# A diffusion backbone kernel on one core: row products dealt differently, context keys normed by head pairs, a tile closed in halves, buffers in another order

## What is computed

```python
for l in range(DEPTH):                       # l = 0: conv and spatial gating; l = 1: conformer and attention
    ada_x = (silu(c) @ w_ada[l] + b_ada[l])  # six vectors of 1024: shift, scale, gate, twice
    hx = modulate(rms_norm(x, norm1_g[l]), ada_x[0], ada_x[1])
    yx = mixer(hx, hc, w_in[l], w_out[l], ...)
    x = x + ada_x[2] * yx
    h2 = modulate(rms_norm(x, norm2_g[l]), ada_x[3], ada_x[4])
    x = x + ada_x[5] * peer(h2, wq[l], subkeys[l], u_tab[l], v_tab[l])
    # layer 0 does the same for the context stream

def diff_attend(q, k, v, lam):               # 4 heads of 2 x 64 keys, 128 values each
    s = einsum('bqhmd,bkhmd->bhmqk', q, k) * 64 ** -0.5
    p = softmax(s)
    return einsum('bhqk,bkhe->bqhe', p[:, :, 0] - lam * p[:, :, 1], v)

def peer(h, wq, subkeys, u_tab, v_tab):      # per token: 8 heads x 16 of 16384 experts
    idx, g = top16_of_products(h @ wq, subkeys)
    act = gelu(einsum('td,thkd->thk', h, u_tab[idx]))
    return einsum('thk,thkd->td', g * act, v_tab[idx])
```

## Time and profile before

| | before |
|---|---|
| time, median of 3 runs (lowest, highest) | 2312.71 us (2308.45, 2313.47) |
| the profiled execution's own time | 2306.4 us |
| its span | 2304.6 us |
| busy: PE, DVE, POOL, ACT | 2060.9, 1597.9, 997.0, 953.3 us |
| moved by DMA | 943.22 MB, mean 409 GB/s |
| of it by gathers (queue q0) | 805.36 MB |

### The profile page before, as it was taken

How to read it: one execution, slowest core, us unless ns; L and a number is a source line. 1 busy time by engine, 2 the same in 40 slices (tenths; PEclk the granted TensorE clock), 3 DMA queues, 4 the chain that set the end, 5 groups by cost and what they waited for, 6 DMA issues and landing times.

```text
span 2304.6 us, 23920 instructions
## 1 busy us (share of the span) xinstructions
PE 2060.9 (89%) x6960; PEld 1126.1 (49%) x6960; DVE 1597.9 (69%) x3904; ACT 953.3 (41%) x2795; POOL 997.0 (43%) x868
## 2 busy tenths in 40 slices
PE   8998998999998888988999998798799978888887
PEld 7785554555564444444554554346546423333222
DVE  3865778967766668888866667855686885666654
ACT  2024444543334444444454334533554443444433
POOL 0003444344444544444445445420344545455663
PEclk9999999999999999999999999999899999999999
DMA  9979999999999999999999999986799999999997
GB/s 405 426 296 388 426 420 427 427 426 427 426 427 426 427 426 426 427 426 427 419 426 427 427 427 427 426 314 284 306 425 426 426 427 426 428 426 427 427 427 319
DMA packets 133618, 943.22 MB, mean 409 GB/s; under 512 B 14832, under 2 KB 18544, under 8 KB 19568
## 3 DMA queue, kind: packets, MB, share of 16 engines
q0 software_dynamic: 110592, 805.36, 83.2%
q1 hardware_dynamic: 22896, 136.35, 14.2%
HBM read 940.60 MB, written 1.05 MB: 409 GB/s over the span
## 4 chain that ended last, share of the span: by engine, by line
PE 38%; DMA 34%; DVE 13%; issue 6%; POOL 5%; ACT 3%; SPq 0%; POOLq 0%; DVEq 0%; ACTq 0%
DMA uv<-uv_dram,stage_idx 32%; PE psum L1016 21%; PE psum L819 9%; DVE uv L1619 5%; POOL uv L1090 5%; PE psum L801 4%; PE psum L959 1%; DVE h L1321 1%; DMA uv<-in_dram 1%; DMA uv<-ada_dram 1%; ACT diag L1264 1%; PE psum L991 1%; PE psum L734 1%; ACT small L1260 1%; DVE work L1427 1%
## 5 line engine op out<-in xcount | busy, mean ns | idle before, releaser
L1016 PE MATMUL psum<-uv,diag 128*128 128x512 f32 x3072 | 1438.7, 611 | 185.1 <-ACT diag L1264 176.7
L1090 POOL DMA_INDIRECT uv<-uv_dram,stage_idx x768 | 965.2, 1257 | 1013.3 <-PE psum L1016 773.1
L1619 DVE CUSTOM_DVE_ANT_0 uv<-uv,h 128x1024 f32<-128x1024 f32 x768 | 932.8, 1225 | 521.6 <-DMA uv<-uv_dram,stage_idx 512.2
L1016 PEld LDWEIGHTS psum<-uv,diag 128*128 128x128 f32 x3072 | 567.1, 193 | 943.8 <-issue 522.8
L1258 ACT ACTIVATE small<-small 128x1 f32<-128x1 f32 x768 | 155.1, 202 | 1016.9 <-DVE small L1619 1015.8
L1264 ACT ACTIVATE diag<-const,small 128x128 f32<-128x128 f32 x768 | 308.4, 402 | 25.1
L819 PE MATMUL psum<-hT,wring 128*128 128x256 f32 (+1 forms) x1344 | 270.9, 355 | 0.0
L819 PEld LDWEIGHTS psum<-hT,wring 128*128 128x128 f32 x1344 | 233.5, 191 | 60.8 <-issue 36.4
L1260 ACT ACTIVATE small<-small,gw 128x1 f32<-128x1 f32 x768 | 226.2, 295 | 24.9
L1076 POOL COPY stage_idx<-idx 128x8 uint32<-128x8 uint32 x96 | 31.6, 329 | 264.2 <-DVE idx L1590 263.6
L1110 ACT ACTIVATE work<-psum 128x256 f32<-128x256 f32 (+2 forms) x127 | 48.3, 383 | 130.1 <-PE psum L819 100.6
(11 more groups left out here) (220 smaller groups left out, 1276.9 us busy)
## 6 DMA issues: line engine op xcount, KB each, us to landing
uv<-ada_dram SPq DMA_DIRECT2D x27, 1024.0 KB, 19.3
wring<-wq_dram SPq DMA_DIRECT2D x26, 1024.0 KB, 11.3
wring<-in_dram SPq DMA_DIRECT2D x23, 1024.0 KB, 9.1
uv<-uv_dram,stage_idx POOLq DMA_INDIRECT x768, 21.2
uv<-in_dram SPq DMA_DIRECT2D x11, 1024.0 KB, 23.2
uv<-ada_t_dram SPq DMA_DIRECT2D x10, 1024.0 KB, 25.8
wring<-ada_dram SPq DMA_DIRECT2D x9, 1024.0 KB, 23.0
uv<-out_w_dram SPq DMA_DIRECT2D x4, 1024.0 KB, 21.0
```

The source lines that it names most:

```text
L1016: last = mm(acc[:, b, :], diag[:, s % DIAGS, :], uv[:, s % RING, D + 512 * b:D + 512 * (b + 1)], start=(c == 0), stop=(c == NSEL - 1))
L1090: nc.gpsimd.indirect_dma_start(out=uv[:, r, :], out_offset=None, in_=tables[stage // 2], in_offset=bass.IndirectOffsetOnAxis(ap=places[:, ...
L1619: v.tensor_tensor_reduce(out=uv[:, r, 0:D], in0=uv[:, r, 0:D], in1=h2[:, row_of[stage], t, :], scale=1.0, scalar=0.0, op0=ALU.mult, op1=AL ...
```

## The change

It has five parts.

1. The buffers are allocated in another order, `uv`, `wring`, `x`, `h2`, `hT`, `work`, `vx` and so on by size, `const` and the small ones last. The built program places 2,048 bytes of DMA scratch and four constants of 32 bytes each ahead of the first buffer, in both kernels. So in each partition `uv` stands at byte 93,440 before (a multiple of 256) and at 2,176 after (128 beyond a multiple of 1,024, and of 256); `wring` at 41,664 before (192 beyond a multiple of 256) and at 92,288 after (128 beyond).
2. In the opening the row products are dealt in three parts: 10 among the first 18 steps of the mixer, 10 among the rest with the gates, and 4 among the four steps `out_rows`.
3. In the gap the keys of tile 1 are normed and turned by pairs of heads, each as soon as its block is there; the scores of heads 0 and 1 wait for the first pair alone; `vc1` block 0 stands behind these scores, block 1 behind `value` of head 1, `ada_turn` of pair 8 behind that; `ada` pair 8 stands behind the norm of the context tile; `lam` moves to the end of stage 1.
4. A tile is closed in halves: a new semaphore `half_summed` tells that bank 0 is summed while PE works on bank 1, and `acc_free` counts halves.
5. The result leaves in four stores of 128 x 512 instead of two of 128 x 1024.

```diff
+    rows = [step for layer, first, last in ADA_ROWS for step in ada_rows_of(layer, first, last)]
...
-        + deal(deal(mixing[:-4] + [mixing[-4], gates[0], mixing[-3], gates[1]] + mixing[-2:],
-                    [step for layer, first, last in ADA_ROWS for step in ada_rows_of(layer, first, last)]),
-               ada(0, 10, 12) + ada(1, 0, 3))
-        + deal(out_rows(0, 0), ada(1, 3, 4)) + [("mods", 0, 1)] + rms(0, one) + ada(1, 4, 6)[:2] + norm(0, 1)[:1] + ada(1, 4, 6)[2:]
+        + deal(deal(mixing[:-12], rows[:10]) + deal(mixing[-12:-4] + [mixing[-4], gates[0], mixing[-3], gates[1]] + mixing[-2:],
+                                                    rows[10:-4]), ada(0, 10, 12) + ada(1, 0, 3))
+        + deal(out_rows(0, 0), rows[-4:] + ada(1, 3, 4)) + [("mods", 0, 1)] + rms(0, one) + ada(1, 4, 6)[:2] + norm(0, 1)[:1] + ada(1, 4, 6)[2:]
...
-        2: [root] + rms(1, (1,)) + [("idle", 10), ("ada", 1, 8), ("kc_turn", 2, 0), ("norm_ctx", 2, 1)]
-        + [("kc1", 2, b, 0) for b in range(2)] + [("kc_norm", 2, 1), exp, ("vc1", 2, 0, 0), ("ada_turn", 1, 8), ("kc_turn", 2, 1), ("lam", 2)]
-        + [scores[0], scores[1], smax[0], smax[1], soft[0], soft[1], ("vc1", 2, 1, 0), mix[0]]
-        + [p_turn[0], scores[2], mix[1], value[0], smax[2], soft[2], p_turn[1], scores[3], mix[2], value[1], smax[3], soft[3]]
+        2: [root] + rms(1, (1,)) + [("idle", 10), ("kc_turn", 2, 0), ("norm_ctx", 2, 1), ("ada", 1, 8)]
+        + [("kc1", 2, 0, 0), ("kc_norm", 2, 1, 0), ("kc1", 2, 1, 0), ("kc_turn", 2, 1, 0), ("kc_norm", 2, 1, 1), exp]
+        + [scores[0], scores[1], ("kc_turn", 2, 1, 1), ("vc1", 2, 0, 0), smax[0], smax[1], soft[0], soft[1], mix[0]]
+        + [p_turn[0], scores[2], mix[1], value[0], smax[2], soft[2], p_turn[1], scores[3], mix[2], value[1], ("vc1", 2, 1, 0),
+           ("ada_turn", 1, 8), smax[3], soft[3]]
...
+    placed += spread([("lam", 2)], at + 248, at + 250)
...
-                if c == 0 and T:
-                    pe.wait_ge(acc_free, T)
                 pe.wait_ge(diag_ready, s + 1)
                 for b in range(2):
+                    if c == 0 and T:
+                        pe.wait_ge(acc_free, 2 * T - 1 + b)
                     last = mm(acc[:, b, :], diag[:, s % DIAGS, :], uv[:, s % RING, D + 512 * b:D + 512 * (b + 1)],
                               start=(c == 0), stop=(c == NSEL - 1))
+                    if c == NSEL - 1 and b == 0:
+                        last.then_inc(half_summed, 1)
...
-                sp.wait_ge(x_rows_ready, t + 1)
-                sp.dma_start(A["result"][t], x[:, TT + t, :]).then_inc(out_stored, 16)
+                for b in range(2):
+                    sp.wait_ge(x_rows_ready, 2 * t + b + 1)
+                    sp.dma_start(A["result"][t][:, b * 512:(b + 1) * 512], x[:, TT + t, b * 512:(b + 1) * 512]).then_inc(out_stored, 16)
...
-            def kc_norm(stage, t):
-                dve.wait_ge(*taken[("kc0", "kc1")[t]])
-                heads_sum(kc_rows[t], sq[:, 0, :])
-                heads_scale(kc_rows[t], 1).then_inc(kc_normed, 1)
+            def kc_norm(stage, t, pair=None):
+                dve.wait_ge(*taken[("kc0", "kc1")[t], 1 if pair is None else pair])
+                heads = heads_of(pair)
+                cols = slice(heads[0] * P, (heads[-1] + 1) * P)
+                heads_sum(kc_rows[t][:, cols], sq[:, 0, cols])
+                heads_scale(kc_rows[t][:, cols], 1).then_inc(kc_normed, 1)
...
-                v.tensor_tensor(tmp, acc.rearrange("p a b -> p (a b)"), gate_peer[:, :], ALU.mult).then_inc(acc_free, 1)
-                dve.wait_ge(acc_free, T + 1)
...
+                for b, half in enumerate(halves):
+                    if b == 0:
+                        dve.wait_ge(half_summed, T + 1)
+                    else:
+                        dve.wait_ge(uv_used, RING + (T + 1) * NSEL)
+                    v.tensor_tensor(tmp[:, half], acc[:, b, :], gate_peer[:, half], ALU.mult).then_inc(acc_free, 1)
+                    if stage == 2:
+                        dve.wait_ge(acc_free, 2 * T + b + 1)
+                        v.tensor_tensor(row[:, half], row[:, half], tmp[:, half], ALU.add).then_inc(x_rows_ready, 1)
+                if stage < 2:
+                    dve.wait_ge(acc_free, 2 * T + 2)
+                    link(v.tensor_tensor(row, row, tmp, ALU.add))
```

More of the change, by code:

```diff
@@ L404, in sem @@
             return ctx.enter_context(nc.semaphore(name))
+        uv = sb("uv", [P, RING, 2 * D])
+        wring = sb("wring", [P, WRING, BLK_W])
+        x = sb("x", [P, 2 * TT, D])
+        h2 = sb("h2", [P, 2, TT, D])
+        hT = sb("hT", [P, KC, TOK])
+        work = sb("work", [P, 8704])
+        vx = sb("vx", [P, TT, MIX])
+        wst = sb("wst", [P, 8 * P])
+        gate_mix = sb("gate_mix", [P, D])
+        gate_peer = sb("gate_peer", [P, D])
+        keys = sb("keys", [P, 2, SUB_W])
+        diag = sb("diag", [P, DIAGS, P])
         const = sb("const", [P, W_CONST])
-        wst = sb("wst", [P, 8 * P])
         ones = sb("ones", [P, P])
-        x = sb("x", [P, 2 * TT, D])
         silu_c = sb("silu_c", [P, KC, QW])
@@ L661, in last_in, with heads_of @@
             return end - 1 - (end - 1 - place) % RING
+        def heads_of(pair):
+            return tuple(range(HEADS)) if pair is None else (2 * pair, 2 * pair + 1)
         def tile_of(stage, t):
@@ L859, in step, with turn_heads, kc_turn @@
                     token_major(to_act, hcT[t], like or name, like is None, like is None)
-                    taken[name] = (act_took, to_act.n)
+                    taken[name] = taken[name, b] = (act_took, to_act.n)
                 return step
-            def turn_heads(tile):
+            def turn_heads(tile, heads=tuple(range(HEADS))):
                 bank = to_act.open(pe)
-                for h in range(HEADS):
-                    last = turn(bank[:, h * P:(h + 1) * P], tile[:, h * P:(h + 1) * P], ident)
+                for i, h in enumerate(heads):
+                    last = turn(bank[:, i * P:(i + 1) * P], tile[:, h * P:(h + 1) * P], ident)
                 to_act.fill(last)
-            def kc_turn(stage, t):
-                pe.wait_ge(kc_normed, t + 1)
-                turn_heads(kc_rows[t])
-                n["kT"] = to_act.n
+            def kc_turn(stage, t, pair=None):
+                pe.wait_ge(kc_normed, n.up("kc_normed"))
+                turn_heads(kc_rows[t], heads_of(pair))
+                n["kT", pair] = to_act.n
             def qk_turn(stage, i, t):
@@ L1146, in heads_root, with ctx_root, kc_turn @@
                 root(root_heads[:, :], ms_heads[:, :])
-            def ctx_root(*_):
-                root(root_heads[:, 0:8], ms_heads[:, 0:8])
+            def ctx_root(stage, t, pair=None):
+                g = 2 * len(heads_of(pair))
+                root(root_heads[:, 0:g], ms_heads[:, 0:g])
             def ctx_rows(dst):
                 return lambda stage, b, *_: empty(dst[:, b * BLK:(b + 1) * BLK], BLK)
-            def kc_turn(stage, t):
-                empty(kcT[:, :, t * P:(t + 1) * P], 4 * P, a=HEADS)
+            def kc_turn(stage, t, pair=None):
+                heads = heads_of(pair)
+                empty(kcT[:, heads[0]:heads[-1] + 1, t * P:(t + 1) * P], len(heads) * P, a=len(heads))
             def qk_turn(stage, i, t):
@@ L1624, in close @@
                 stage, t = T // TT, T % TT
-                dve.wait_ge(uv_used, RING + (T + 1) * NSEL)
                 dve.wait_ge(*taken["gate", stage, 1])
-                tmp = h2[:, row_of[stage], t, :]
-                v.tensor_tensor(tmp, acc.rearrange("p a b -> p (a b)"), gate_peer[:, :], ALU.mult).then_inc(acc_free, 1)
-                dve.wait_ge(acc_free, T + 1)
-                row = x[:, tile_of(stage, t), :]
-                done = v.tensor_tensor(row, row, tmp, ALU.add)
-                if stage == 2:
-                    done.then_inc(x_rows_ready, 1)
-                else:
-                    link(done)
+                tmp, row = h2[:, row_of[stage], t, :], x[:, tile_of(stage, t), :]
+                halves = [slice(b * 512, (b + 1) * 512) for b in range(2)]
+                for b, half in enumerate(halves):
[10 more added lines that the diff above has]
+                    link(v.tensor_tensor(row, row, tmp, ALU.add))
             v.memset(ones[:, :], 1.0)
```

23 lines of the change are left out of this document (8 added, 15 removed).

## The result

| | before | changed |
|---|---|---|
| median | 2310.58 us (2307.8 to 2313.47, 4 runs) | 2336.84 us (2335.1 to 2338.68, 4 runs) |
| profiled execution: own time, span | 2306.4, 2304.6 | 2335.98, 2334.2 |
| rate of the full stretches | 424 and 426 GB/s | 418 and 421 GB/s |

The ratio is 1.0114 (95% interval 1.0096 to 1.0131): 26 us slower, where I forecast no change and a range up to 2319. Of the times that I had named, that of the rival with 0.04 (2342) lies nearest.

What follows compares the result with a forecast made beforehand. DMA was taken to bound the kernel, so only time where DMA stands could change. Terms -1.5 + 2.3 - 0.9 = -0.1 gave 2306.3 us profiled, 2312.6 against the runs' median of 2312.7; range 2305 to 2319.

Steps and rivals of the forecast that it cites:

- the rival with 0.04: Gathers into uv: unaligned rows of 8192 bytes each cost 128 bytes more, +29 us, 2342; chance 0.04.
- Buffers: 0 us: New buffer places: loads into wring (428 GB/s) and gathers into uv (427) equally fast, so the new offset costs 0.
- the rule: DMA rule of the Trainium skill: a descriptor not starting at a multiple of 256 B fetches from the multiple below.
- Opening: -1.5 us: Opening: first gather 4.0 us sooner, at 162.5, but five gathers instead of six ahead of the wait, +2.5; net -1.5.
- The first rival's other gain: Opening: last out_rows block spared the 0.50 clock, gathers' wait ends 2.0 us sooner, opening wins 3.5; rival's chance 0.25.
- Gap: +2.3 us: Gap: first exponentials 1.3 us sooner, but copies hold those of head 3, losing that and 2.3 us more.
- The rival of the falling clock: Gap: PE stands 3.3 us and its clock falls; gap costs +7.3, whole +4.9, 2317.6; chance 0.18.
- its own condition: Gap: the clock rival decides when PE runs at 0.50 from p_turn of head 0 through vc1 block 1.
- The reason given that waits of 2.5 us do not bring 0.50: Gap: argument against the falling clock; the trace before showed waits of 2.5 us at clock 1.00.
- Tail: -0.9 us: Tail: closing in halves saves 0.6 us, a last store half as large 0.3 us; bounds -0.4 and -1.3.
- 5.0 us after PE's last slot: Tail: sign to look for, the last store in two halves and the end 5.0 us after PE's last slot.
- the sum -0.1: Whole kernel: opening -1.5, gap +2.3 and tail -0.9, with buffers 0, add to -0.1 us.

Runs made afterwards that it cites:

- e1: The kernel before with only the change's order of buffers (uv at byte 2176, 128 beyond a multiple of 256): 2339.35 us, ratio to before 1.0126.
- e4: The kernel before with a 128-byte buffer (ci) placed just ahead of uv, so uv starts 128 beyond a multiple of 256: 2339.98 us, ratio to before 1.0122.
- e7: The kernel before with the 64-byte prec moved behind uv, so uv starts 192 beyond a multiple of 256: 2338.65 us, 1.0134.
- e8: The kernel before with the 96-byte stage_idx placed ahead of uv, so uv starts 96 beyond a multiple of 256: 2339.22 us, 1.0137.
- e3: The changed kernel with a 128-byte buffer (ci) ahead of uv, so uv and wring start at multiples of 256: 2307.55 us, ratio to before 0.9984.
- e5: e3 with the steps of the gap as in the kernel before (one key norm of four heads): 2306.37 us, 0.9988.
- e6: e3 with vc1 block 1 back ahead of the turning of head 0, under the first exponentials; keys still normed by pairs: 2304.17 us, 0.9984.
- e12: e6 with ci and ada_c (896 bytes) ahead of uv, so uv, wring, x, h2, hT, work start at multiples of 1024: 2304.89 us, 0.9979.
- e9: The kernel before with the 64-byte prec ahead of wring, moving wring to a multiple of 256 while uv stays: 2307.46 us, 0.9993.

## Why the prediction was wrong

**Buffers: 0 us. This step failed**, and it alone put the time out of the range. The words were: "at both places the rate is the same, so it should be at 128 beyond too". The rates were read from windows of 7 us and 80 us, and the first can't carry the comparison. The landings in the same trace, 2.481 us apart for 2.447, would have spoken for the rule, as the earlier trace rows seemed to speak against it. The term is +28 us (e1 and e4: +29). The rival had the place, the sign and nearly the size (+29), and I gave it 0.04 on the strength of the faulty reading. That its size fits is in part luck: it took the cost of a row from the 128 bytes of this offset, and e7 and e8 show the same cost at 192 and at 96. A cost that falls on 768 transfers needs evidence at 1% before it is put aside.

**Opening: -1.5 us. Right, within the scatter.** `out_rows` at 123.83 (123.3 forecast), last addition to the end at 141.06 (140.4), the turning at 144.84 (144.3), the first gather at 163.02 (162.5), five gathers ahead. DMA stands some 4 us before 150 (share 0.97), as foreseen. The 21st gather lands 1.7 us earlier in the changed kernel; in the kernels with `uv` at a multiple of 256 and the changed opening (e2, e3, e5, e6, e12) it lands at 227.6 to 230.1, with the old one at 230.5 and 232.3 (before, e9). That is -2 us, with a scatter as large. With `uv` off and the old opening (e1, e4, e7, e8) it lands at 231.2 to 233.3, 2.4 to 4.5 us behind the changed kernel. The first rival's other gain here did not come: the last block behind the wait again ran partly at 0.50 (5.22 us).

**Gap: +2.3 us. Right in mechanism, too small.** The first exponentials came 1.5 us sooner (1.3 forecast), those of head 3 were held by the two copies, and block 1 was the step that did it (e6). But head 3 came 15.7 us behind head 0, not 13.7, and the gap cost +4.0. The rival of the falling clock named what was missing: PE stood 3.11 us (3.3 forecast) and ran at 0.50 behind it, from `p_turn` of head 0 on. By its own condition it did not fully decide: `vc1` block 1 ran at full clock (3.62 us), so it cost some 2 us (15.7 for 13.7) and not 5. The reason given that waits of 2.5 us do not bring 0.50 held in that one trace: behind the same 2.52 us, PE's clock fell in e4, e5, e8 and e9. Against before as a group of traces rather than one, the changed gap is 2 to 6 us dearer.

**Tail: -0.9 us. Right:** -1.0 from the last landing, -1.1 from PE's last slot. The end "5.0 us after PE's last slot" that I gave as a sign does not follow from this sum: it was 5.6 before (2304.6 less 2299.0), so 4.7 was due, and it came at 4.4.

**Pieces that add up.** Without the buffers, the sum -0.1 would have stood: e2, the changed kernel on the old buffers, is at 0.9995 (0.9986 to 1.0005). That is no proof of each piece: the gap was 1.7 us off in the changed kernel and 2.6 in e2, and the time does not resolve that.

## What to carry to other kernels

When a kernel is bound by DMA, the start of every buffer that DMA fills is part of its design: align it to 256 bytes, and look the address up in the built program, where scratch and constants ahead of the first buffer can spoil an order that looks aligned in the source. Before you set aside an effect of 1%, ask whether the view could have shown it: compare landings or hundreds of transfers, not one short window. And where a step moves out of the shadow of another, look for the engine that now stands there, and for the copy that holds the queue behind it.

## What the runs showed of the hardware

- A gather or load into SBUF costs 0.038 us more for each MB (128 rows of 8192 bytes) when its rows start 96, 128 or 192 beyond a multiple of 256: 2.621 to 2.623 for 2.583 us of spacing in stage 2. A start at a multiple of 1024 is no better than one at a multiple of 256 (e12, e6). Other row sizes were not run.
- The same work of PE behind much the same wait goes at either clock from one program to the next. The last `out_rows` block took 3.72 us behind 3.33 us of standing in e3, with no stretch at 0.50; behind 3.64 us in e2 it took 6.28, but behind only 2.87 us in e8 it took 5.41, both partly at 0.50. Timeline of e3 and of e2:

```profile
177.34 3.72 PE L807 MATMUL psum<-uv,work 128*128 128x256 f32 x16 [3.33 <-DVE work L1540]
```

```profile
177.69 6.28 PE L807 MATMUL psum<-uv,work 128*128 128x256 f32 x16 [3.64 <-DVE work L1540]
```

- Likewise the gap of before takes 75.2 to 75.3 us in three traces and 77.5 to 77.7 in four. The difference is 6.8 us at a granted clock of 0.50 behind the exponentials of head 3, which the four have and the three have not, behind the same wait of 2.52 us. One profile of each kernel can't tell 2 us there; why the clock falls in one and not in the other is left open.
